# One matmul for both token parts in the last 64 key tiles, the first 64 key tiles split by GpSimd alone, and the first value parts made during the last key tile

## The chip, the cores and the metric

The kernel runs on one core of one Trainium2 chip. The metric is the device time in microseconds; lower is better. TensorE does the matmuls, VectorE (DVE) and ScalarE (ACT) the elementwise work, GpSimd (POOL) one kind of elementwise work, and SyncE (SP) issues the DMAs.

## The reference

One decoder block for 256 tokens of width 1024: a mixer (gated convolution and dilated attention), then PEER, a retrieval of single-neuron experts. The change is in PEER:

```python
def peer(xn, w_q, sub_keys, u_tab, v_tab):
    ...
        q = (xc @ w_q).reshape(TOKEN_CHUNK, PEER_HEADS, 2, half)
        s = jnp.einsum('thpd,hpnd->thpn', q, sub_keys).astype(jnp.float32)
        top_s, top_i = lax.top_k(s, PEER_TOPK)
        cand = top_s[:, :, 0, :, None] + top_s[:, :, 1, None, :]
        best_s, best_c = lax.top_k(cand.reshape(...), PEER_TOPK)
        ...
        e = i1 * PEER_N_KEYS + i2
        gate = jax.nn.softmax(best_s, axis=-1).astype(xc.dtype)
        h = jnp.einsum('thkd,td->thk', u_tab[e], xc)
        act = jax.nn.gelu(h, approximate=False) * gate
        return jnp.einsum('thk,thkd->td', act, v_tab[e])
```

There are 128 x 128 experts, each with one row of 1024 numbers in `u_tab` (its key) and one in `v_tab` (its value).

## The kernel before, in words

The kernel gathers nothing. It multiplies the tokens by all 16,384 keys, applies gelu, multiplies by a dense matrix of gates that is zero where an expert was not picked, and multiplies by all values. Keys and values come as 128 tiles each, of 128 x 1024 numbers (512 KB): 128 key tiles (the stage `U0`), then 128 value tiles (the stage `V0`). Ahead of them stand 76 tiles of the mixer and of the query projection (the front).

**Precision.** Every product of 32-bit numbers is made from parts: a weight is `hi + lo`, a token vector is `nrm_hi + nrm_lo`, and a tile's result is `hi*nrm_hi + hi*nrm_lo + lo*nrm_hi`. For each tile ACT copies `raw` to `hi` (`split_hi`, L310), and then POOL or DVE makes `lo = raw - hi` (`split_lo`, L323). `by_dve` says which: DVE takes every fourth tile up to tile 67 of the keys, and every second from there (from `G_SHARED`); POOL takes the others. `raw`, `hi` and `lo` are rings of four tiles (`RING`). A new `raw` tile is loaded when the `lo` of the tile four before is made, and `hi` of tile n+3 (`LEAD` is 3) is made after the matmuls of tile n-1, which used the same slot.

**A key tile** (`u_tile`, by `product`, L1055) is 24 matmuls of 256 columns (the 256 tokens): eight units of the 1024 dimensions, three products each. The result is 128 keys x 256 tokens in the first half of bank 4 or 5, by turns. ACT makes gelu of it into `act` (L573), and tile n+2 waits until gelu of tile n has freed the bank (`gelu_done`).

**During the first 64 key tiles** DVE picks the experts: `top_step` runs sorts (L857, L859, L862) and, per chunk of 128 tokens, one tensor of 2048 candidate sums per partition (L871) and two lookups, each of two products of 2048 elements and a sum (L881, L886, L888). The splits of `lo` that are DVE's stand between these steps in its program, at the places that `tile_of` gives.

**During the last 64 key tiles and the first 64 value tiles** the gates are made for 8 tokens at a time, 32 groups per half: DVE builds one-hot matrices (`one_hots`: `eqB` L965, `ohA` L967, `ohB` L971), TensorE multiplies them (`gates`, L1283, 16 matmuls of 64 columns ahead of every second tile), and DVE multiplies `act` by the result (`multiply`, L983). `gate_body` is DVE's loop over four tiles.

**A value tile** (`v_tile`, L1326) is 12 matmuls of 512 columns, in which the `act` tile, again in two parts, is the loaded side. ACT makes its `nrm_hi` (`a_split`, L598) and DVE its `nrm_lo` (`low_part`, L990). The two parts take the first four blocks of the arrays that held the token parts during the key tiles.

There is no scheduler: each engine runs its program in the order in which it is written, and the engines meet at semaphores. A wait holds up all that is behind it on its engine.

## Time and profile before

| | us |
|---|---|
| median of 3 runs (1066.76 to 1069.2) | 1067.68 |
| the profiled execution | 1069.04 |
| its span, first to last instruction | 1067.3 |
| TensorE busy | 1049.8 |
| DVE busy | 751.4 |
| POOL busy | 514.0 |
| ACT busy | 509.7 |

The busy time is the time in which an engine had at least one instruction under way. Matmuls overlap each other in the records, so the pace of TensorE is read from the distance between two starts and not from the duration of one. The stages lie so: front to 291, key tiles from 298 to 694 (the last 64, with gates, from 488), value tiles with gates from 694 to 888, value tiles without gates to the end. L12 is line 12 of the kernel before.

### The profile page before, as it was taken

To read this page: it belongs to the slowest core of one execution; us is meant where nothing else is said; L and a number is where in the kernel's file an instruction comes from. 1 tells how busy PE (TensorE), PEld (TensorE's weight loads), DVE (VectorE), ACT (ScalarE), POOL (GpSimd) and SP (SyncE) were. 2 spreads that over 40 slices of the span, in tenths; PEclk is the share of its full clock that TensorE was granted. 3 is DMA by queue.
4 is the path that set the end of the run, shared out by engine and by line. 5 is a ranking of instruction groups with operands and counts; after the bars stand their busy time and mean duration, and the time that the engine had idled before them with its cause. 6 is when DMAs were issued, how large, how long until landed. Compare 5 with 4: busy or idle time off the path is not lost.

```text
span 1067.3 us, 21882 instructions
## 1 busy us (share of the span) xinstructions
PE 1049.8 (98%) x7850; PEld 961.8 (90%) x7850; DVE 751.4 (70%) x1232; ACT 509.7 (48%) x798; POOL 514.0 (48%) x216
## 2 busy tenths in 40 slices
PE   8999999999999998999999999999999999999998
PEld 6999898999999998999999999978887777888886
DVE  5375868744079899918555555599999997777775
ACT  5453667545454443454444444444444444444553
POOL 3654452654646694964344333444434434444442
PEclk8999999999999998999999999999999999999999
DMA  5864342644535544465554455545554555666662
GB/s 195 267 209 139 125 149 84 216 160 141 182 133 183 191 148 166 140 214 174 167 172 158 161 173 168 166 158 177 177 172 162 177 177 178 197 196 188 190 194 97
DMA packets 52258, 181.91 MB, mean 170 GB/s; under 512 B 5851, under 2 KB 9051, under 8 KB 52092
## 3 DMA queue, kind: packets, MB, share of 16 engines
q1 hardware_dynamic: 52220, 181.41, 52.0%
q8 instruction: 24, 0.39, 0.1%
q14 instruction: 14, 0.11, 0.0%
HBM read 177.97 MB, written 3.41 MB: 170 GB/s over the span
## 4 chain that ended last, share of the span: by engine, by line
PE 91%; DVE 7%; issue 1%; ACT 1%; DMA 0%; SPq 0%; ACTq 0%; DVEq 0%
PE bank L1055 49%; PE bank L1326 33%; PE bank L1283 3%; PE bank L1136 2%; DVE lo L323 1%; PE bank L1065 1%; PE bank L1149 1%; PE bank L1263 1%; DVE gsig L829 1%; DVE prob L748 1%; DMA relx<-rel_bias 0%; DVE act L881 0%; DVE act L886 0%; DVE act L871 0%; PE bank L1243 0%
## 5 line engine op out<-in xcount | busy, mean ns | idle before, releaser
L323 POOL TENSOR_TENSOR lo<-raw,hi 128x1024 fp32r<-128x1024 f32 x202 | 511.1, 2535 | 538.5 <-ACT hi L310 538.1
L310 ACT CAST hi<-raw 128x1024 fp32r<-128x1024 f32 x332 | 347.9, 1048 | 200.9 <-PE bank L1326 189.8
L1055 PE MATMUL bank<-nrm_hi,hi 128*128 128x256 f32 x1504 | 433.4, 288 | 7.5 <-DVE lo L323 5.1
L1055 PE MATMUL bank<-nrm_lo,hi 128*128 128x256 f32 x1504 | 428.1, 285 | 0.0
L1055 PE MATMUL bank<-nrm_hi,lo 128*128 128x256 f32 x1504 | 427.9, 285 | 0.0
L1055 PEld LDWEIGHTS bank<-nrm_hi,hi 128*128 128x128 f32 x1504 | 291.1, 194 | 12.9 <-issue 7.7
L1055 PEld LDWEIGHTS bank<-nrm_lo,hi 128*128 128x128 f32 x1504 | 291.4, 194 | 0.1
L1055 PEld LDWEIGHTS bank<-nrm_hi,lo 128*128 128x128 f32 x1504 | 291.1, 194 | 0.0
L323 DVE TENSOR_TENSOR lo<-raw,hi 128x1024 fp32r<-128x1024 f32 x130 | 173.6, 1336 | 111.0 <-ACT hi L310 110.5
L990 DVE TENSOR_TENSOR nrm_lo<-act,nrm_hi 128x256 fp32r<-128x256 f32 x128 | 151.0, 1182 | 51.2 <-ACT nrm_hi L598 51.1
L1326 PE MATMUL bank<-hi,nrm_hi 128*128 128x512 f32 x512 | 160.6, 395 | 0.7 <-ACT nrm_hi L598 0.7
L1326 PE MATMUL bank<-hi,nrm_lo 128*128 128x512 f32 x512 | 158.9, 391 | 0.3 <-DVE nrm_lo L990 0.3
L1326 PE MATMUL bank<-lo,nrm_hi 128*128 128x512 f32 x512 | 158.0, 390 | 0.0
L573 ACT ACTIVATE act<-bank 128x256 f32 x128 | 49.1, 384 | 218.0 <-PE bank L1055 217.9
L1326 PEld LDWEIGHTS bank<-hi,nrm_lo 128*128 128x128 f32 x512 | 95.1, 188 | 22.9 <-DVE nrm_lo L990 3.7
L1326 PEld LDWEIGHTS bank<-lo,nrm_hi 128*128 128x128 f32 x512 | 96.1, 188 | 20.2
L1326 PEld LDWEIGHTS bank<-hi,nrm_hi 128*128 128x128 f32 x512 | 93.7, 188 | 18.7 <-issue 0.8
L983 DVE SCALAR_TENSOR_TENSOR act<-bank,act 128x512 f32 (+1 forms) x64 | 43.9, 685 | 83.6 <-PE bank L1283 83.6
L971 DVE TENSOR_TENSOR ohB<-eqB,parts 128x1024 f16<-128x1024 f16 x64 | 59.2, 925 | 0.0
L967 DVE TENSOR_TENSOR ohA<-iota_nk,keys 128x1024 f16<-128x1024 f16 x64 | 52.5, 820 | 0.0
L598 ACT CAST nrm_hi<-act 128x256 fp32r (+1 forms) x128 | 51.2, 402 | 0.1
L689 DVE SCALAR_TENSOR_TENSOR bank<-u_pad,prm,bank 128x256 f32<-128x256 f32 x116 | 46.7, 481 | 0.0
(172 smaller groups left out, 764.8 us busy)
## 6 DMA issues: line engine op xcount, KB each, us to landing
raw<-u_tiles SPq DMA_DIRECT2D x128, 512.0 KB, 3.4
raw<-v_tiles SPq DMA_DIRECT2D x128, 512.0 KB, 3.4
raw<-front SPq DMA_DIRECT2D x76, 512.0 KB, 3.4
toeplitz<-prob SPq DMA_DIRECT2D x12, 192.0 KB, 4.4
bias<-toeplitz SPq DMA_DIRECT2D x12, 128.0 KB, 4.1
resid<-x_t SPq DMA_DIRECT2D x2, 512.0 KB, 4.5
qk<-sub_keys SPq DMA_DIRECT2D x1, 1024.0 KB, 6.8
y<-act SPq DMA_DIRECT2D x2, 512.0 KB, 2.6
```

What stands on the lines that cost most here:

```text
L310: act_e.copy(hi[:, s, :], raw[:, s, :]).then_inc(hi_ready, 1)
L323: eng.tensor_tensor(lo[:, s, :], raw[:, s, :], hi[:, s, :].bitcast(F32), ALU.subtract)\
L573: a.activation(act[:, it * 4 + (base_i + j), :], bank[4 + j % 2][:, 0:T], ACT.Gelu).then_inc(gelu_done, 1)
L598: a.copy(nrm_hi[:, (base_i + j) % RING, :], act[:, it * 4 + (base_i + j), :]).then_inc(a_hi, 1)
L689: dve.scalar_tensor_tensor(out=acc[:, b, :] if w == TAPS - 1 else part_sum, in0=src, scalar=wt, in1=part_sum, op0=ALU.mult, op1=ALU.add).t ...
L967: dve.tensor_tensor(ohA[:, g % 2], every_pair(iota_nk[:, :, :], NK), at(keys[:, 0, t], NK), ALU.is_equal).then_inc(spread, 1)
L971: dve.tensor_tensor(ohB[:, g % 2].rearrange("p a i n b -> p (a i) n b"), eqB[:, g % 2].unsqueeze(2).broadcast_to([P, TOK // PAIR, 2, HALF, ...
L983: dve.scalar_tensor_tensor(out=av, in0=gv, scalar=1.0 / GATE_SCALE, in1=av, op0=ALU.mult, op1=ALU.mult)\
L990: dve.tensor_tensor(nrm_lo[:, s, :], act[:, it * 4 + (base_i + j), :], nrm_hi[:, s, :].bitcast(F32), ALU.subtract).then_inc(a_lo, 1)
L1055: ins = pe.matmul(dst, w_[:, s, u * P:(u + 1) * P], x_[:, k, :], start=first and i == 0 and p_ == 0, stop=last and i == n - 1 and p_ == 2)
L1283: ins = pe.matmul(bank[6 + g][:, q * HALF:(q + 1) * HALF], ohA[:, g, q // PAIR, :, q % PAIR], ohB[:, g, q // PAIR, i, :, q % PAIR], start= ...
L1326: ins = pe.matmul(bank[2 * c + half][:, :], a_[:, j, c * P:(c + 1) * P], v_[:, j, half * 512:(half + 1) * 512], start=False, stop=stop and ...
```

## The change

1. **Wide key tiles.** The two token parts are interleaved in one array `nrm`, so that one matmul of 512 columns makes `hi*nrm_hi` (left half of the bank) and `hi*nrm_lo` (right half). `lo*nrm_hi` is a matmul of 256 columns into the left half. This is done in the last 64 key tiles only (`wide_tile`): 8 matmuls of 512 and 8 of 256 columns instead of 24 of 256. The halves must then be added: ACT copies the right half to `half_sum` (`copy_cross`), DVE adds the left half (`add_halves`), and ACT makes gelu of the sum (`gelu_sum`). The bank of tile n is free for tile n+2 when DVE has added (`added`).
2. **Order on ACT** in these tiles: copy of tile n, gelu of tile n-1, `split_hi` of tile n+3. Before it was `split_hi` of tile n+3, then gelu of tile n.
3. **GpSimd splits** all of the first 64 key tiles of the loop (key tiles 3 to 66); DVE none of them.
4. **The turn to the values.** During the last key tile ACT makes `nrm_hi` and DVE `nrm_lo` of the first value tile (semaphore `blocks_free`), and DVE makes the first two one-hot groups of the second half in the last round of the first half instead of behind it. `eqB` has one buffer instead of two.

```diff
         raw = sb("raw", [P, RING, D])
         hi = sb("hi", [P, RING, D], F32R)
         lo = sb("lo", [P, RING, D], F32R)
-        nrm_hi = sb("nrm_hi", [P, KB, T], F32R)
-        nrm_lo = sb("nrm_lo", [P, KB, T], F32R)
+        nrm = sb("nrm", [P, KB, 2, T], F32R)
+        nrm_hi, nrm_lo = nrm[:, :, 0, :], nrm[:, :, 1, :]
...
 
         parts = sb("parts", [P, T // PAIR, 2, PAIR], F16)
         ohA = sb("ohA", [P, 2, TOK // PAIR, NK, PAIR], F16)
-        eqB = sb("eqB", [P, 2, TOK // PAIR, HALF, PAIR], F16)
+        eqB = sb("eqB", [P, TOK // PAIR, HALF, PAIR], F16)
+        half_sum = sb("half_sum", [P, 2, T])
...
         def by_dve(base, j):
 
+            if U0 + LEAD <= base + j < G_SHARED:
+                return False
             return slot_of(base, j) == 3 or (base + j >= G_SHARED and slot_of(base, j) == 1)
...
             a.wait_ge(pick_ready, 2)
-            with a.Fori(0, HALF // RING) as it:
-                for j in range(RING):
-                    split_hi(a, U0 + HALF + LEAD, it, j)
-                    gelu(HALF, it, j)
+            def copy_cross(it, j):
+
+                a.wait_ge(pe_step, it * 4 + (S_U + HALF + j + 1))
+                a.wait_ge(gelu_done, it * 4 + (HALF + j - 1))
+                a.copy(half_sum[:, j % 2, :], bank[4 + j % 2][:, T:2 * T]).then_inc(crossed, 1)
+
+            def gelu_sum(base, it, j):
+
+                a.wait_ge(added, it * 4 + (base + j + 1))
+                a.activation(act[:, it * 4 + (HALF + base + j), :], half_sum[:, (base + j) % 2, :], ACT.Gelu)\
+                 .then_inc(gelu_done, 1)
 
             def a_split(base_i, it, j):
 
                 wait(a, pe_step, it * 4 + (S_V + base_i + j - 3))
                 a.copy(nrm_hi[:, (base_i + j) % RING, :], act[:, it * 4 + (base_i + j), :]).then_inc(a_hi, 1)
 
+            def key_round(it, first=False, last=False):
+                for j in range(RING):
+                    if last and j == RING - 1:
+                        a.wait_ge(gated, GROUPS_N)
+                        a.wait_ge(blocks_free, 1)
+                        a_split(0, 0, 0)
+                    copy_cross(it, j)
+                    if not (first and j == 0):
+                        gelu_sum(-1, it, j)
+                    split_hi(a, U0 + HALF + LEAD, it, j)
+
+            key_round(0, first=True)
+            with a.Fori(1, HALF // RING - 1) as it:
+                key_round(it)
+            key_round(HALF // RING - 1, last=True)
+            gelu_sum(HALF - 1, 0, 0)
...
             for half in range(2):
-                a.wait_ge(gated, GROUPS_N * (half + 1))
-                a_split(HALF * half, 0, 0)
+                if half:
+                    a.wait_ge(gated, GROUPS_N * 2)
+                    a_split(HALF, 0, 0)
...
             for i in range(HALF):
-                if by_dve(U0 + LEAD, i):
-                    split_lo(dve, U0 + LEAD, 0, i)
                 for n, tile in enumerate(tile_of):
...
                 wait(dve, gate_mm, n - 1)
+                wait(dve, spread, n * 2)
...
-                dve.tensor_tensor(eqB[:, g % 2], every_pair(iota_nk[:, half * HALF:(half + 1) * HALF, :], HALF),
...
+
+            def add_halves(it, j):
+
+                dve.wait_ge(crossed, it * 4 + (j + 1))
+                dve.tensor_tensor(half_sum[:, j % 2, :], bank[4 + j % 2][:, 0:T], half_sum[:, j % 2, :], ALU.add)\
+                   .then_inc(added, 1)
...
 
@@ -1003,14 +1036,19 @@
                         multiply(half, it, j // 2)
                     elif not last:
                         one_hots(half, it, 2 + j // 2)
+                    elif half == 0:
+                        one_hots(1, 0, j // 2)
                     if by_dve(base + LEAD, j):
                         split_lo(dve, base + LEAD, it, j)
+                    if half == 0:
+                        if last and j == RING - 1:
+                            low_part(0, 0, 0)
+                        add_halves(it, j)
...
             for half in range(2):
-                one_hots(half, 0, 0)
-                one_hots(half, 0, 1)
-                if half == 1:
-                    low_part(0, 0, 0)
+                if half == 0:
+                    one_hots(0, 0, 0)
+                    one_hots(0, 0, 1)
                 gate_body(half, 0, first=True)
                 with dve.Fori(1, HALF // RING - 1) as it:
...
+            def wide_tile(it, j, last=False):
+
+                b = bank[4 + j % 2]
+                if isinstance(it, int) and it == 0 and j < 2:
+                    pe.wait_ge(gelu_done, HALF + j - 1)
+                else:
+                    pe.wait_ge(added, it * 4 + (j - 1))
+                wait_lo(pe, U0 + HALF, it, j)
+                for k in range(KB):
+                    unit = slice(k * P, (k + 1) * P)
+                    pe.matmul(b[:, :], hi[:, j, unit], nrm[:, k, :, :].rearrange("p a t -> p (a t)"),
+                              start=k == 0, stop=False, skip_group_check=True)
+                    ins = pe.matmul(b[:, 0:T], lo[:, j, unit], nrm_hi[:, k, :],
+                                    start=False, stop=k == KB - 1, skip_group_check=True)
+                    if last and k == RING - 1:
+                        ins.then_inc(blocks_free, 1)
+                ins.then_inc(pe_step, 1)
...
-            def u_and_gates(it):
+            def u_and_gates(it, last=False):
                 for j in range(RING):
                     if j % 2 == 0:
                         gates(0, it, j // 2)
-                    u_tile(HALF, it, j)
+                    wide_tile(it, j, last and j == RING - 1)
 
             u_and_gates(0)
-            with pe.Fori(1, HALF // RING) as it:
+            with pe.Fori(1, HALF // RING - 1) as it:
                 u_and_gates(it)
```

The order on **ACT** in the last 64 key tiles. Before, one tile and the start of the next, from the loop (`L573` is gelu, `L310` is `split_hi` of tile n+3; REGISTER_ALU and ISA rows carry waits and addresses):

```order
L310 CAST hi<-raw 128x1024 [waits pe_step,raw_in0]
L572 REGISTER_ALU
L573 ISA [waits pe_step]
L573 ACTIVATE act<-bank 128x256
L310 CAST hi<-raw 128x1024 [waits pe_step,raw_in1]
```

Of the change, the last two tiles (`L598` is the copy of tile n, `L603` gelu of the sum of tile n-1, `L312` is `split_hi` of tile n+3, `L609` is `a_split` of the first value tile):

```order
L598 COPY half_sum<-bank 128x256 [waits gelu_done,pe_step]
L603 ACTIVATE act<-half_sum 128x256 [waits added]
L312 CAST hi<-raw 128x1024 [waits pe_step,raw_in1]
L609 CAST nrm<-act 128x256 [waits pe_step,blocks_free,gated]
L598 COPY half_sum<-bank 128x256 [waits gelu_done,pe_step]
L603 ACTIVATE act<-half_sum 128x256 [waits added]
L312 CAST hi<-raw 128x1024 [waits pe_step,raw_in2]
L603 ACTIVATE act<-half_sum 128x256 [waits added]
```

`split_hi` of tile n+3 now stands behind the copy of tile n, which waits until the matmuls of tile n are done; before it waited only for those of tile n-1.

The order on **DVE** in the same tiles. Before, an even and an odd tile, the first round of `gate_body` (`L983` is `multiply`, `L323` is `split_lo` of tile n+3, then a one-hot group):

```order
L983 SCALAR_TENSOR_TENSOR act<-bank,act 128x64x8 [waits gate_mm,gelu_done]
L323 TENSOR_TENSOR lo<-raw,hi 128x1024 [waits hi_ready]
L965 TENSOR_TENSOR eqB<-iota_nk,keys 128x512 [waits gate_mm]
L967 TENSOR_TENSOR ohA<-iota_nk,keys 128x1024
L971 TENSOR_TENSOR ohB<-eqB,parts 128x1024 [waits second]
```

Of the change, an even and an odd tile (`L1010` is `multiply`, `L327` is `split_lo`, `L1023` is `add_halves`):

```order
L1010 SCALAR_TENSOR_TENSOR act<-bank,act 128x64x8 [waits gate_mm]
L327 TENSOR_TENSOR lo<-raw,hi 128x1024 [waits hi_ready]
L1023 TENSOR_TENSOR half_sum<-bank,half_sum 128x256 [waits crossed]
L992 TENSOR_TENSOR eqB<-iota_nk,keys 128x512 [waits spread,gate_mm]
L994 TENSOR_TENSOR ohA<-iota_nk,keys 128x1024
L998 TENSOR_TENSOR ohB<-eqB,parts 128x1024 [waits second]
L1023 TENSOR_TENSOR half_sum<-bank,half_sum 128x256 [waits crossed]
```

In every even tile the addition stands behind `split_lo` of tile n+3, which waits for `split_hi` of tile n+3 on ACT; in every odd tile it stands behind a one-hot group.

The order on **DVE** in the first 64 key tiles, at the two lookups of the second chunk. Before:

```order
L881 TENSOR_TENSOR act<-act,iota 128x2048 [waits chain]
L886 TENSOR_TENSOR act<-act 128x2048 [waits chain]
L888 TENSOR_REDUCE act<-act 128x128 [waits chain]
L323 TENSOR_TENSOR lo<-raw,hi 128x1024 [waits hi_ready,chain]
L881 TENSOR_TENSOR act<-act,iota 128x2048
L886 TENSOR_TENSOR act<-act 128x2048 [waits chain]
L888 TENSOR_REDUCE act<-act 128x128 [waits chain]
L916 TENSOR_TENSOR act<-act 128x128 [waits chain]
L323 TENSOR_TENSOR lo<-raw,hi 128x1024 [waits hi_ready] x2
```

Of the change, the same steps:

```order
L909 TENSOR_TENSOR act<-act,iota 128x2048 [waits chain]
L914 TENSOR_TENSOR act<-act 128x2048 [waits chain]
L916 TENSOR_REDUCE act<-act 128x128 [waits chain]
L909 TENSOR_TENSOR act<-act,iota 128x2048 [waits chain]
L914 TENSOR_TENSOR act<-act 128x2048 [waits chain]
L916 TENSOR_REDUCE act<-act 128x128 [waits chain]
L944 TENSOR_TENSOR act<-act 128x128 [waits chain]
```

The splits between the steps are gone, and with them every wait of DVE for ACT in this stage until the gates' softmax.

## Rows read from the trace of the kernel before

**Rows 1.** The page, part 4: the chain that ended last, by engine.

```profile
PE 91%; DVE 7%; issue 1%; ACT 1%; DMA 0%; SPq 0%; ACTq 0%; DVEq 0%
```

**Rows 2.** Chain in order of time, two pairs of key tiles: start, duration us.

```profile
598.87 5.83 PE bank L1055 x48
605.19 5.83 PE bank L1055 x48
```

**Rows 3.** Timeline, 404 to 424: start, duration us, engine, line [idle before <-releaser].

```profile
412.40 2.72 DVE L323 TENSOR_TENSOR lo<-raw,hi 128x1024 fp32r<-128x1024 f32 x1
...
415.26 0.55 PE L1055 MATMUL bank<-nrm_hi,hi 128*128 128x256 f32 x1 [5.10 <-DVE lo L323]
...
415.83 0.41 PE L1055 MATMUL bank<-nrm_hi,lo 128*128 128x256 f32 x1
416.04 0.41 PE L1055 MATMUL bank<-nrm_hi,hi 128*128 128x256 f32 x1
```

**Rows 4.** Windows, TensorE alone: stretch, length, busy (instructions), granted clock, DMA.

```profile
210.00:215.00 5.00, 3.70 (x31) 1.00 0.50 183
410.00:420.00 10.00, 4.90 (x24) 0.73 0.31 107
420.00:430.00 10.00, 10.00 (x80) 0.93 0.40 155
```

**Rows 5.** Timeline, POOL, DVE and ACT in the first 64 key tiles.

```profile
302.27 2.41 POOL L323 TENSOR_TENSOR lo<-raw,hi 128x1024 fp32r<-128x1024 f32 x1 [9.23 <-ACT hi L310]
...
370.85 2.29 DVE L881 TENSOR_TENSOR act<-act,iota 128x2048 f32<-128x2048 f32 x1
...
371.38 10.80 POOL L323 TENSOR_TENSOR lo<-raw,hi 128x1024 fp32r<-128x1024 f32 x3 [3.36 <-ACT hi L310]
...
373.17 4.38 DVE L886 TENSOR_TENSOR act<-act 128x2048 f32<-128x2048 f32 x1
377.59 2.29 DVE L888 TENSOR_REDUCE act<-act 128x128 f32<-128x2048 f32 x1
...
402.07 1.05 ACT L310 CAST hi<-raw 128x1024 fp32r<-128x1024 f32 x1
```

**Rows 6.** Timeline, 598 to 605.5: one pair of key tiles with gates.

```profile
598.50 0.38 ACT L573 ACTIVATE act<-bank 128x256 f32 x1 [1.56 <-PE bank L1055]
...
598.78 1.04 ACT L310 CAST hi<-raw 128x1024 fp32r<-128x1024 f32 x1
...
599.86 1.23 DVE L323 TENSOR_TENSOR lo<-raw,hi 128x1024 fp32r<-128x1024 f32 x1 [0.15 <-ACT hi L310]
...
601.00 0.42 DVE L965 TENSOR_TENSOR eqB<-iota_nk,keys 128x512 f16<-128x512 f16 x1
...
604.30 0.28 PE L1055 MATMUL bank<-nrm_lo,hi 128*128 128x256 f32 x1
...
604.42 0.28 PE L1055 MATMUL bank<-nrm_hi,lo 128*128 128x256 f32 x1
...
604.83 0.38 ACT L573 ACTIVATE act<-bank 128x256 f32 x1 [1.56 <-PE bank L1055]
...
605.03 0.36 PE L1055 MATMUL bank<-nrm_hi,hi 128*128 128x256 f32 x1
...
605.23 0.28 PE L1055 MATMUL bank<-nrm_lo,hi 128*128 128x256 f32 x1
```

**Rows 7.** Timeline, TensorE in the value tiles, merged by two.

```profile
959.93 0.62 PE L1326 MATMUL bank<-hi,nrm_hi 128*128 128x512 f32 x2
...
962.65 0.62 PE L1326 MATMUL bank<-hi,nrm_hi 128*128 128x512 f32 x2
```

**Rows 8.** Line L793, DVE adding from a bank: duration ns min/median/max.

```profile
L793 DVE TENSOR_TENSOR o_lo<-bank,o_hi x6: 415/424/425, 175.9 to 183.2; 128x256 fp32r<-128x256 f32 x6
```

**Rows 9.** Timeline, 686 to 702: the turn from keys to values.

```profile
693.11 0.66 PE L1283 MATMUL bank<-ohB,ohA 128*128 128x64 f16 x16
...
693.92 0.71 ACT L598 CAST nrm_hi<-act 128x256 fp32r<-128x256 f32 x2
...
694.47 0.70 PE L1326 MATMUL bank<-hi,nrm_hi 128*128 128x512 f32 x2 [0.71 <-ACT nrm_hi L598]
```

**Rows 10.** Waits of TensorE's loads: us in total, times, longest.

```profile
PEld bank L1326 <- DVE nrm_lo L990: 3.7, 13, 0.7
```

More of the change, by code:

```diff
@@ L268, in hybrid_block @@
         sc_ready = sem("sc_ready")
-        gelu_done = sem("gelu_done")
+        crossed, added, gelu_done = sem("crossed"), sem("added"), sem("gelu_done")
         top_done, gexp, gate_ready, pick_T, pick_ready = [sem(s) for s in (
@@ L272, in hybrid_block @@
         second, spread, gate_mm, gated = sem("second"), sem("spread"), sem("gate_mm"), sem("gated")
+        blocks_free = sem("blocks_free")
         a_hi, a_lo = sem("a_hi"), sem("a_lo")
@@ L963, in every_pair @@
                     return x.unsqueeze(1).broadcast_to([P, TOK // PAIR, m, PAIR])
-                dve.tensor_tensor(eqB[:, g % 2], every_pair(iota_nk[:, half * HALF:(half + 1) * HALF, :], HALF),
+                dve.tensor_tensor(eqB[:, :, :, :], every_pair(iota_nk[:, half * HALF:(half + 1) * HALF, :], HALF),
                                   at(keys[:, 1, t], HALF), ALU.is_equal).then_inc(second, 1)
@@ L972, in one_hots @@
                     ohB[:, g % 2].rearrange("p a i n b -> p (a i) n b"),
-                    eqB[:, g % 2].unsqueeze(2).broadcast_to([P, TOK // PAIR, 2, HALF, PAIR]),
+                    eqB[:, :, :, :].unsqueeze(2).broadcast_to([P, TOK // PAIR, 2, HALF, PAIR]),
                     parts[:, two, :, :].rearrange("p a i b -> p (a i) b").unsqueeze(2)
@@ L1310, in u_and_gates @@
                         gates(0, it, j // 2)
-                    u_tile(HALF, it, j)
+                    wide_tile(it, j, last and j == RING - 1)
             u_and_gates(0)
-            with pe.Fori(1, HALF // RING) as it:
+            with pe.Fori(1, HALF // RING - 1) as it:
                 u_and_gates(it)
+            u_and_gates(HALF // RING - 1, last=True)
             def v_tile(base_i, it, j, stop=False):
```

## The prediction

> **What bounds the kernel now.** I read the chain that ended last first: TensorE holds 91% of it and DVE 7% [rows 1]. So a change pays where it shortens TensorE's own work or takes away a wait of TensorE, and it costs where it makes one. The chain in order of time shows the stage of the change as a regular beat: two key tiles and one group of gates every 6.32 us [rows 2]. In the timeline of that stage a matmul of 256 columns starts 0.12 after the one before, so a tile is 24 x 0.12 = 2.88 us; the gates add 0.12 to 0.49 of starts and 0.08 on the second matmul behind them, 0.57 in all, and 2 x 2.88 + 0.57 is the 6.33 of the beat [rows 2, 6]. TensorE has no wait there. A matmul of 512 columns costs less for its columns: 12 of them take 2.72 us, 0.227 each [rows 7].
>
> In the first 64 key tiles the timeline shows TensorE waiting once, 5.10 us, for a split that DVE made late, behind its sorts [rows 3]. After it the matmuls start 0.21 apart instead of 0.12 [rows 3]: the granted clock is 0.73 and 0.93 of full over two stretches of 10 us, which is 6.8 us at 1.2 GHz instead of 2.4 [rows 4].
>
> **The first 64 key tiles: what goes.** The late split is no longer DVE's, so the 5.1 us wait goes. With it goes the low clock: 6.8 us at half rate do the work of 6.8 x 0.12 / 0.213 = 3.8 us, a loss of 3.0 at most; a part of it lies in the wait, and I take 2.7. Together -7.8.
>
> **The first 64 key tiles: what comes.** POOL needs 2.41 us for a split alone, inside the 2.88 of a tile [rows 5]. But it does not run alone. When DVE's product L881 started at 370.85, POOL's splits went from 371.38 to 382.18, 10.80 for three. DVE's next product L886, issued 1.79 after POOL, took 4.38, while the sum L888 took its 2.29 beside POOL [rows 5]. I read this as taking turns: a DVE product of two arrays in SBUF and a split of POOL never run together, and each product takes its 2.28 from POOL. 10.80 less what is left of L881 (1.76) and one product (2.28) leaves 6.76 for three splits, 2.25 each.
>
> The Trainium skill says the same (SBUF — State Buffer, Who interferes with whom): a DVE instruction with two SBUF inputs and a GpSimd one that reads SBUF block each other fully, and a reduction never contends. By that rule the new addition, with one input in PSUM, stays out of it; the trace agrees as far as its rows go.
>
> Until now POOL had one free slot in four tiles to catch up; it loses it. DVE's work is no longer spread out by its splits, so the products come close together. First stretch (two lookups of the first chunk, then L871): five products, 11.4 us of POOL's time, within 22.7 us (each product followed by a split, and two sums). TensorE uses 22.7 / 2.88 = 7.9 tiles in it, 7.9 x 2.40 = 19.0 of POOL. 30.4 into 22.7 leaves POOL 7.7 behind. What it may be behind: `hi` of 402.07 is ready at 403.12, a split alone would be done at 405.6, and TensorE came to that tile at 415.26 - 5.10 = 410.16: 4.5 us with the handover [rows 3, 5]. So TensorE waits 3.2. Second stretch (lookups of the second chunk): four products and small steps, 10.0, within 18; 6.25 tiles x 2.40 = 15; behind by 7.0, wait 2.5. Sum 5.7. With 2.25 for a split it is 2.0 + 1.6 = 3.6. The waits come in pieces of a split or less with matmuls between. A stretch with 1.3 of 5 us idle kept the clock at 1.00 [rows 4], so I charge no clock; if it falls in both stretches, 2 x 2.7 more. I take +5.7, bounds 3.6 and 11.
>
> **The last 64 key tiles.** TensorE's own work: a wide tile is 8 x 0.227 + 8 x 0.120 = 2.78, 0.107 less than now; the beat could be 6.11 instead of 6.32.
>
> The Trainium skill (TensorE: Matmul & The Clock Gate, Back-to-back issue gap) gives a gap of columns / 2.4 + 2.5 ns, with which eight matmuls fewer would save 20 ns a tile. The trace does not agree: 120 and 227 ns are 13 ns over the columns' time. By the page the beat could only be 6.28, and in the sum below a wide tile would be 0.09 longer, +2.7 us in all; I go by the rows.
>
> Whether TensorE keeps its pace depends on the bank. Tile n+2 waits for the addition of tile n. For an even tile the way there is, from the last matmul's start: to ACT 0.41 (604.42 to 604.83); copy of the right half, next instruction after 0.28 (598.50 to 598.78) [rows 6]; gelu of tile n-1 from SBUF, between 0.28 and half of the two casts' 0.71, I take 0.30 [rows 9]; `split_hi` 1.04; to DVE 0.04; `split_lo`, which stands ahead of the addition, 1.14 (599.86 to 601.00) [rows 6]; the addition 0.42, as L793, the same form [rows 8]; to TensorE 0.14 (415.12 to 415.26) [rows 3]. Sum 3.77. The tile itself takes 8 x 0.227 + 7 x 0.12 + 0.08 = 2.73 from its first to its last start. An even tile can follow an even tile after 6.50 us, not 6.11: TensorE would stand still for 0.39 in each pair, behind the gates. Against now that is +0.18 a pair, 31 times: +5.6. Bounds: 0.15 either way on the chain, +1 to +10.
>
> Odd tiles don't bind. DVE ends the even addition about 0.5 after the odd tile is done, the one-hots take 1.6 more, the addition 0.4, so the bank is free some 2.6 after the tile's end, and tile n+2 starts later than 3.1. Behind the waiting addition on DVE stand only the one-hots and `multiply`, which have a pair's time to spare. POOL's split of the odd tiles ends about 0.7 after the even tile's end, a microsecond before DVE's split begins, so the two don't meet. The loads from HBM (same number, same size) follow the splits, with more than 5 us in hand.
>
> **The turn and the rest.** Behind the last gates TensorE started the values after 1.36 (693.11 to 694.47), where gates alone take 0.49 [rows 6, 9]. Parts and one-hots are now ready: -0.9. The work moved into the last round (one cast, one subtraction, two one-hot groups) fills DVE where no split or one-hot of its own was due. One buffer for `eqB` costs nothing, since other work stands between two groups. In the values DVE is late now and then, 3.7 us in 13 waits of the loads [rows 10], most of it hidden; it may move by 1 either way, and I put 0.
>
> **Sum.** -7.8 + 5.7 + 5.6 - 0.9 = +2.6 on the profiled 1069.04, which lies 1.4 above the median: 1067.7 + 2.6 = 1070.2 (rounded). About 0.2%, 2.1 us, is what a measurement can tell here.
>
> **The rivals.**
> 1. The bank's chain doesn't bind. It would have to be 3.38 or less. For it: all its terms are small, and ACT and DVE are half idle; against it: each term is in a row, and the order of both programs puts two splits into it. Then -7.8 + 5.7 - 6.6 - 0.9 = -9.6: 1058. Chance 0.12.
> 2. POOL keeps up, because it gets two turns for one of DVE during the sums. For it: DVE waits for POOL too, which spreads its products. Then -5.7 on the forecast: 1064.5. Chance 0.12.
> 3. The other way: POOL's waits lower the clock in both stretches, since they lie close together: +5.4, 1075.6. It decides from a stretch in which TensorE is idle as in the 5.1 us wait. Chance 0.12.
> 4. A wide tile has the smaller saving, because a matmul of 256 columns behind one of 512 does not keep 0.12. Then +2.7, 1073. Chance 0.06.
> The forecast as worked out, 1066 to 1074, has 0.58.
>
> **How the numbers follow.** The forecast is slightly over the bound to slower; of its 0.58 I give 0.38 to slower, 0.18 to same, 0.02 to faster. Rival 1 is faster, rival 2 is faster by 0.06 and the same by 0.06, rivals 3 and 4 are slower but for 0.02. Faster 0.20, same 0.26, slower 0.54. The range 1062 to 1076 leaves out rival 1 and the far side of rival 3.
>
> **What would show it.** The beat of the key tiles with gates: 6.50 (right), 6.11 (rival 1). In each pair a wait of TensorE's wide matmul for DVE's addition, about 0.4. In the first 64 key tiles no wait of 5 us, but some four to six of 0.5 to 1.8 for POOL's `lo`, in two clusters, around 380 and 428, with the clock at 1.00. POOL busy for 90% and more of those stretches. At the turn, 0.5 from gates to values. The prediction is wrong if ACT makes `split_hi` before the copy's turn comes in practice, if additions run in less than 0.42, or if POOL's splits stay on time.

## The result, and the profile after

| | before | this kernel |
|---|---|---|
| median of 22 runs each, us | 1069.21 (1066.76 to 1074.11) | 1072.16 (1070.29 to 1076.24) |
| ratio, 95% interval | | 1.0024 [1.0013, 1.0035] |
| span of the profiled execution, us | 1067.3 | 1070.7 |

The kernel became slower by 0.24%, on the side and about by the size of the forecast (+2.6 us). Three of the terms behind the sum were off, though, and partly made up for each other. The stages, read from the first product matmul of the key tiles, from the starts of the groups of gates, and from the last instruction:

| stage, us | before | after | difference | forecast |
|---|---|---|---|---|
| first 64 key tiles (to the first gates) | 193.04 | 189.10 | -3.94 | -2.1 |
| last 64 key tiles (first gates to the 33rd) | 202.45 | 206.79 | +4.34 | +5.6 |
| turn and values with gates (33rd to 64th gates) | 189.37 | 192.32 | +2.95 | -0.9 |
| all else | 482.4 | 482.5 | +0.1 | 0 |

The page of the kernel after, parts 1 and 4, against [rows 1]:

```profile
PE 1051.4 (98%) x7338; PEld 930.2 (87%) x7338; DVE 757.8 (71%) x1280; ACT 530.5 (50%) x862; POOL 551.2 (51%) x232
PE 79%; issue 8%; DVE 5%; ACT 4%; POOL 3%; DVEq 1%; DMA 0%; ACTq 0%; SPq 0%; POOLq 0%
```

TensorE's share of the chain fell from 91% to 79%: other engines now stand in it, POOL between 364 and 426 in the first 64 key tiles, ACT and DVE all through the last 64. The waits of TensorE, its matmuls first, then its loads (us in total, times, longest):

```profile
PE bank L1093 <- POOL lo L327: 3.1, 4, 1.3
...
PE bank L1383 <- DVE nrm L1017: 1.6, 3, 0.8
...
PE bank L1325 <- DVE half_sum L1023: 0.4, 2, 0.2
```

```profile
PEld bank L1383 <- DVE nrm L1017: 10.4, 33, 1.3
```

The second row looks small, and so does the third; the beats tell more. Gates are shown busy for 0.66 us, though the next matmul can start 0.50 after their start (693.56 and 694.06 below), so most of a wait behind gates does not appear as idle time.

**First 64 key tiles.** Timeline, TensorE's four waits for POOL (idle time in brackets):

```profile
376.96 0.48 PE L1093 MATMUL bank<-nrm,hi 128*128 128x256 f32 x2 [1.28 <-POOL lo L327]
...
386.15 0.47 PE L1093 MATMUL bank<-nrm,hi 128*128 128x256 f32 x2 [0.32 <-POOL lo L327]
...
421.19 0.47 PE L1093 MATMUL bank<-nrm,hi 128*128 128x256 f32 x2 [0.25 <-POOL lo L327]
...
425.58 0.48 PE L1093 MATMUL bank<-nrm,hi 128*128 128x256 f32 x2 [1.28 <-POOL lo L327]
```

and POOL, then DVE's products of a lookup, in the first of the two stretches:

```profile
357.17 47.75 POOL L327 TENSOR_TENSOR lo<-raw,hi 128x1024 fp32r<-128x1024 f32 x16 [0.61 <-ACT hi L312]
```

```profile
363.42 2.29 DVE L916 TENSOR_REDUCE act<-act 128x128 f32<-128x2048 f32 x1
365.74 4.43 DVE L909 TENSOR_TENSOR act<-act,iota 128x2048 f32<-128x2048 f32 x1
370.20 4.38 DVE L914 TENSOR_TENSOR act<-act 128x2048 f32<-128x2048 f32 x1
374.62 2.29 DVE L916 TENSOR_REDUCE act<-act 128x128 f32<-128x2048 f32 x1
```

POOL works 47.75 us without a gap, 2.98 a split, where it needs 2.41 alone [rows 5] and TensorE uses a tile in 2.88. The products take 4.4 and the sums 2.29, as in [rows 5]. The waits come in two clusters, around 380 and 423, four in all.

**Last 64 key tiles.** Timeline of one pair, ACT and then DVE, against [rows 6]:

```profile
600.32 0.37 ACT L598 COPY half_sum<-bank 128x256 f32<-128x256 f32 x1 [1.76 <-PE bank L1327]
600.59 0.42 ACT L603 ACTIVATE act<-half_sum 128x256 f32 x1
600.90 1.04 ACT L312 CAST hi<-raw 128x1024 fp32r<-128x1024 f32 x1
...
606.82 0.37 ACT L598 COPY half_sum<-bank 128x256 f32<-128x256 f32 x1 [1.80 <-PE bank L1327]
```

```profile
601.98 1.23 DVE L327 TENSOR_TENSOR lo<-raw,hi 128x1024 fp32r<-128x1024 f32 x1 [2.44 <-ACT hi L312]
603.12 0.42 DVE L1023 TENSOR_TENSOR half_sum<-bank,half_sum 128x256 f32<-128x256 f32 x1
```

TensorE's wide matmul starts behind it at 603.67. From the copy: 0.27 to gelu, 0.31 to `split_hi`, 1.08 to `split_lo`, 1.14 to the addition, 0.55 to TensorE, then 3.15 for the tile and the handover to the next copy: 6.50. DVE was idle for 2.44 before its split, so it was not overloaded; it stood at the wrong wait.

**The turn and the values.** Timeline at the turn, TensorE, then DVE, against [rows 9]:

```profile
693.56 0.66 PE L1339 MATMUL bank<-ohB,ohA 128*128 128x64 f16 x16
694.06 0.70 PE L1383 MATMUL bank<-hi,nrm 128*128 128x512 f32 x2
...
696.07 1.21 PE L1383 MATMUL bank<-hi,nrm 128*128 128x512 f32 x4 [0.85 <-DVE nrm L1017]
```

```profile
695.60 0.42 DVE L1017 TENSOR_TENSOR nrm<-act,nrm 128x256 fp32r<-128x256 f32 x1
695.94 0.42 DVE L1023 TENSOR_TENSOR half_sum<-bank,half_sum 128x256 f32<-128x256 f32 x1
697.20 1.37 DVE L1017 TENSOR_TENSOR nrm<-act,nrm 128x256 fp32r<-128x256 f32 x1 [0.85 <-ACT nrm L609]
```

The values do start 0.50 after the gates, not 1.36. But TensorE stops again four matmuls later: `nrm_lo` of the first value tile stands behind the second one-hot group on DVE and comes at 696. Then the loop, POOL and DVE:

```profile
743.08 2.53 POOL L327 TENSOR_TENSOR lo<-raw,hi 128x1024 fp32r<-128x1024 f32 x1 [3.62 <-ACT hi L312]
749.21 2.54 POOL L327 TENSOR_TENSOR lo<-raw,hi 128x1024 fp32r<-128x1024 f32 x1 [3.60 <-ACT hi L312]
```

```profile
742.14 1.21 DVE L327 TENSOR_TENSOR lo<-raw,hi 128x1024 fp32r<-128x1024 f32 x1
743.27 2.62 DVE L1017 TENSOR_TENSOR nrm<-act,nrm 128x256 fp32r<-128x256 f32 x1
...
749.42 2.62 DVE L1017 TENSOR_TENSOR nrm<-act,nrm 128x256 fp32r<-128x256 f32 x1
```

DVE has no idle time here and needs 6.15 a pair. In it, `low_part` takes 2.62 where it takes 0.42 alone [its row at 695.60]: it starts 0.19 behind a split of POOL and ends 0.28 behind it. TensorE could do a pair in 6.05.

### The profile page after: what moved, and what is told of

Read it like the earlier page. It is cut to its first block, busy times and chain, and to the rows that moved or that the text cites. A ratio compares the mean times of both kernels' runs of the same rounds, so it can differ in the third digit from the quotient of the medians.

```text
span 1070.7 us, 21144 instructions
## 1 busy us (share of the span) xinstructions
PE 1051.4 (98%) x7338; PEld 930.2 (87%) x7338; DVE 757.8 (71%) x1280; ACT 530.5 (50%) x862; POOL 551.2 (51%) x232
## 4 chain that ended last, share of the span: by engine, by line
PE 79%; issue 8%; DVE 5%; ACT 4%; POOL 3%; DVEq 1%; DMA 0%; ACTq 0%; SPq 0%; POOLq 0%
PE bank L1383 32%; PE bank L1093 28%; PE bank L1325 7%; PE bank L1327 3%; ACT hi L312 3%; POOL lo L327 3%; PE bank L1174 2%; PE bank L1339 2%; DVE half_sum L1023 1%; PE bank L1103 1%; PE bank L1187 1%; PE bank L1301 1%; DVE nrm L1017 1%; DVE gsig L857 1%; DVE prob L776 1%
## 5 line engine op out<-in xcount | busy, mean ns | idle before, releaser
L327 POOL TENSOR_TENSOR lo<-raw,hi 128x1024 fp32r<-128x1024 f32 x218 | 548.3, 2525 | 504.7 <-ACT hi L312 504.4
L312 ACT CAST hi<-raw 128x1024 fp32r<-128x1024 f32 x332 | 347.5, 1047 | 202.1 <-PE bank L1383 191.0
L1093 PE MATMUL bank<-nrm,hi 128*128 128x256 f32 x1984 | 363.5, 286 | 5.4 <-POOL lo L327 3.1
L1093 PEld LDWEIGHTS bank<-nrm,hi 128*128 128x128 f32 x1984 | 312.0, 194 | 11.3 <-issue 3.4
L1383 PE MATMUL bank<-hi,nrm 128*128 128x512 f32 x1024 | 285.3, 395 | 1.6 <-DVE nrm L1017 1.6
L1093 PE MATMUL bank<-nrm,lo 128*128 128x256 f32 x992 | 282.2, 284 | 0.0
L327 DVE TENSOR_TENSOR lo<-raw,hi 128x1024 fp32r<-128x1024 f32 x114 | 144.1, 1264 | 135.8 <-ACT hi L312 135.7
L1383 PEld LDWEIGHTS bank<-hi,nrm 128*128 128x128 f32 x1024 | 187.4, 188 | 45.8 <-DVE nrm L1017 10.4
L1017 DVE TENSOR_TENSOR nrm<-act,nrm 128x256 fp32r<-128x256 f32 x128 | 180.8, 1414 | 50.0 <-ACT nrm L609 50.0
L1093 PEld LDWEIGHTS bank<-nrm,lo 128*128 128x128 f32 x992 | 192.1, 194 | 0.0
L1325 PE MATMUL bank<-nrm,hi 128*128 128x512 f32 x512 | 184.1, 403 | 3.4 <-DVE half_sum L1023 0.4
L1383 PE MATMUL bank<-lo,nrm 128*128 128x512 f32 x512 | 158.4, 390 | 0.0
L1327 PE MATMUL bank<-nrm,lo 128*128 128x256 f32 x512 | 143.1, 279 | 0.0
L1325 PEld LDWEIGHTS bank<-nrm,hi 128*128 128x128 f32 x512 | 96.1, 188 | 28.6 <-issue 3.6
L1383 PEld LDWEIGHTS bank<-lo,nrm 128*128 128x128 f32 x512 | 96.1, 188 | 20.3
L1327 PEld LDWEIGHTS bank<-nrm,lo 128*128 128x128 f32 x512 | 96.7, 189 | 0.0
L598 ACT COPY half_sum<-bank 128x256 f32<-128x256 f32 x64 | 23.8, 372 | 95.9 <-PE bank L1327 95.9
L609 ACT CAST nrm<-act 128x256 fp32r (+1 forms) x128 | 51.2, 402 | 0.0
```

The costliest lines, as they stand in the source:

```text
L312: act_e.copy(hi[:, s, :], raw[:, s, :]).then_inc(hi_ready, 1)
L327: eng.tensor_tensor(lo[:, s, :], raw[:, s, :], hi[:, s, :].bitcast(F32), ALU.subtract)\
L609: a.copy(nrm_hi[:, (base_i + j) % RING, :], act[:, it * 4 + (base_i + j), :]).then_inc(a_hi, 1)
L1017: dve.tensor_tensor(nrm_lo[:, s, :], act[:, it * 4 + (base_i + j), :], nrm_hi[:, s, :].bitcast(F32), ALU.subtract).then_inc(a_lo, 1)
L1093: ins = pe.matmul(dst, w_[:, s, u * P:(u + 1) * P], x_[:, k, :], start=first and i == 0 and p_ == 0, stop=last and i == n - 1 and p_ == 2)
L1325: pe.matmul(b[:, :], hi[:, j, unit], nrm[:, k, :, :].rearrange("p a t -> p (a t)"), start=k == 0, stop=False, skip_group_check=True)
```

## The experiments

All are compared with runs of the kernel before on the same chip. Stages are read as in the table above. The start of the first key tile moves by up to 3 us from one profile to another, so spans are not compared, stages are.

### The addition ahead of the split, and POOL alone with the splits

**e1.** In every even tile DVE adds before it splits:

```diff
-                    if by_dve(base + LEAD, j):
-                        split_lo(dve, base + LEAD, it, j)
                     if half == 0:
                         if last and j == RING - 1:
                             low_part(0, 0, 0)
                         add_halves(it, j)
+                    if by_dve(base + LEAD, j):
+                        split_lo(dve, base + LEAD, it, j)
```

> The changed kernel with one line moved: in every even key tile DVE adds the halves before it makes the lo of tile n+3, not behind it. My theory: the bank of an even tile comes free through copy, gelu, split of hi, split of lo and addition, 3.77 us, and that chain sets the beat of 6.50 us a pair. With the addition first the chain is copy and addition alone, about 1.4 us, TensorE sets the beat at 6.11, and the stage is 12 us shorter: ratio to before about 0.991, 1060 us. Rival: the beat is set by something else that comes to 6.50 as well (the copies on ACT, or DVE's whole work in a pair): then the beat stays at 6.4 or more and the time moves by under 2 us.

Measured: 1063.41 us, ratio 0.9931 [0.9905, 0.9957]; last 64 key tiles 196.27, every beat 6.13 or 6.14, the other stages as in the changed kernel within 0.3. Timeline, DVE:

```profile
603.06 0.42 DVE L1023 TENSOR_TENSOR half_sum<-bank,half_sum 128x256 f32<-128x256 f32 x1 [1.18 <-ACT half_sum L598]
604.32 1.23 DVE L327 TENSOR_TENSOR lo<-raw,hi 128x1024 fp32r<-128x1024 f32 x1 [0.83 <-ACT hi L312]
```

The addition now follows the copy of 602.66 by 0.40 instead of 2.80. The chain of the even tiles was the cost, and nothing else in that stage was: 10.5 us lie in the order of two instructions, where 12 were expected.

**e2.** The kernel before, with the third part of the change alone:

```diff
         def by_dve(base, j):
 
+            if U0 + LEAD <= base + j < G_SHARED:
+                return False
...
             for i in range(HALF):
-                if by_dve(U0 + LEAD, i):
-                    split_lo(dve, U0 + LEAD, 0, i)
```

> The kernel before with one part of the change alone: POOL makes every lo of key tiles 3 to 66, DVE none. The two profiles put the first gates 3.9 us earlier in the changed kernel (486.8 against 490.7). My theory: this part gives that alone, 3.9 us less in all, ratio 0.996, with about four waits of TensorE for POOL's lo, 3 us in sum, clock at 1.00. Rival: what is won is given back in the value tiles, since DVE comes to them in another state: ratio 1.000 within 0.001.

Measured: 1064.82 us, ratio 0.9956 [0.9939, 0.9974]; first 64 key tiles 189.10, four waits for POOL's `lo`, 3.2 us together, clock 1.00 throughout the stretch. The gain of this part stands alone, and the rest of its kernel is as before (202.45 and 189.34), the beats of the value tiles too. So what the changed kernel loses in the values comes from the other parts of the change.

### How much the lock costs in the first half

The lock is what the prediction calls taking turns: a product of DVE with two inputs in SBUF and a split of POOL don't run together.

**e7.** In six of the eight products of the lookups DVE works on an eighth of the elements (the first chunk's first lookup keeps its size), so the picked experts are not the reference's:

```diff
+                    n = PH * TOPK if (c, w) == (0, 0) else TOPK
...
+                    h = PH if (c, w) == (0, 0) else 1
+                    link(dve.tensor_tensor(e4[:, 0:h], e4[:, 0:h], tf[:, 0:h], ALU.mult))
```

> The changed kernel with six of the eight large products of DVE's lookups cut to an eighth of their size (the first lookup keeps its size; the picked experts are then not those of the reference). It shows what POOL's waits for these products cost in the first 64 key tiles. My theory: the products hold POOL up for 2.28 us each, so with them gone TensorE's waits for POOL's lo, 3.1 us in four pieces in the changed kernel, fall to 0.5 or less, and the stage from the first key tile to the first gates takes 186.0 to 186.5 instead of 189.1. Rival: POOL is late because of all its splits together or because of the loads behind them: then 188.5 or more.

Measured, one run: 1068.37; first 64 key tiles 185.03 instead of 189.10, and no wait for POOL's `lo`. The cost of POOL as the only splitter is DVE's products in its way: 4.07 us.

### The turn

**e3.** `nrm_lo` of the first value tile and the last addition ahead of the second one-hot group:

```diff
                     elif half == 0:
+                        if j == RING - 1:
+                            low_part(0, 0, 0)
+                            add_halves(it, j)
                         one_hots(1, 0, j // 2)
...
```

> The changed kernel with the last key tile's work on DVE in another order: the nrm_lo of the first value tile and the addition of the last key tile stand before the second one-hot group, not behind it. After the change the value tiles with gates took 199.4 us against 195.5, at a beat of 6.15 instead of 6.05. Theory A: DVE is the bound of that stage at 6.15 a pair; before, it came into the stage with a lead of about 2 us that lasted for 21 pairs; the change spends the lead at the turn, where DVE stands idle for 1.7 us and TensorE waits 0.85. With the new order TensorE does not wait at the turn and DVE has 1.7 us of lead more: the value stage takes 197 us or less, time 2 to 3 us less, ratio to before about 1.000. Rival B: the beat of 6.15 comes from the position of POOL's splits against DVE's, not from a lead: only the 0.85 at the turn goes, ratio 1.0016.

**e4.** e1 and e3 together.

> The addition first in every key tile and the new order at the turn, both. If the two effects are apart they add: 12 and 2 to 3 us less than the changed kernel, about 1057 us, ratio to before 0.989. If the faster key tiles bring DVE later into the value stage (it has less idle time at a beat of 6.11), a part of it is given back there: 1059 to 1060.

Measured: e3 1072.34, ratio 1.0028 [1.0010, 1.0045], values with gates 193.49; e4 1060.62, ratio 0.9908 [0.9883, 0.9934], 196.26 for the last 64 key tiles and 191.82 for the values. As a cure e3 failed. Timeline of e3, POOL, DVE and TensorE:

```profile
693.31 2.41 POOL L327 TENSOR_TENSOR lo<-raw,hi 128x1024 fp32r<-128x1024 f32 x1 [4.00 <-ACT hi L312]
693.35 2.91 DVE L998 TENSOR_TENSOR ohB<-eqB,parts 128x1024 f16<-128x1024 f16 x1
...
696.19 2.56 DVE L1017 TENSOR_TENSOR nrm<-act,nrm 128x256 fp32r<-128x256 f32 x1
698.80 1.65 PE L1385 MATMUL bank<-hi,nrm 128*128 128x512 f32 x3 [3.16 <-DVE nrm L1017]
```

The one-hot product and then `nrm_lo` of the second value tile each landed behind a split of POOL, and TensorE waited 3.16 us; 3.4 us of low clock followed at 698.8. But what came then told more than the cure would have: 20 beats of 6.05 to 6.08, and 6.15 only after them. The kernel before has the same (behind a first beat of 6.90, 20 beats of 6.05 or 6.06, then 6.09 to 6.19), while the changed kernel has 6.15 from the third beat on. A lead of DVE would hide its pace in this way, at 0.10 a pair. That DVE's pace was 6.15 in the fast beats too can be read in the kernel before, in whose timeline two runs of `multiply` lie 6.15 apart while TensorE's beat is 6.05:

```profile
744.20 0.68 DVE L983 SCALAR_TENSOR_TENSOR act<-bank,act 128x512 f32 x1
...
750.35 0.68 DVE L983 SCALAR_TENSOR_TENSOR act<-bank,act 128x512 f32 x1
```

e4 has the same order at the turn as e3, but its wait there is 0.74 us and not 3.16, and it has no fast beats: 6.11 to 6.20 from the third on. The order of e3 alone builds no lead.

### The values: which work stands behind POOL

**e5.** In the second half DVE multiplies in the odd tiles, ahead of `low_part`, so that POOL's split meets `multiply` first, which has one input in PSUM, and `low_part` later:

```diff
+                    if half == 1 and j % 2:
+                        multiply(half, it, j // 2)
                     if half == 1 and not (last and j == RING - 1):
                         low_part(1, it, j)
                     if j % 2 == 0:
-                        multiply(half, it, j // 2)
+                        if half == 0:
+                            multiply(half, it, j // 2)
```

> The changed kernel with DVE's multiply of the value tiles moved from ahead of the even tile's split of lo to behind it, just ahead of the odd tile's nrm_lo. In the trace of the changed kernel that nrm_lo takes 2.6 us instead of 0.4, since POOL's split is under way; multiply reads a bank and runs beside POOL (0.61). Theory A (DVE is the bound of the value tiles with gates at 6.15 a pair, 2.2 of it behind POOL): the wait swallows multiply, DVE's round is 5.54, TensorE sets the beat at 6.05 in all pairs but the first two, the 32 groups take 189.5 instead of 192.3, time 2.8 less: ratio to before 1.000. Rival C: POOL's split starts when TensorE and ACT let it, so DVE waits for its end wherever multiply stands, or another DVE step is caught instead: beat 6.15 stays, ratio 1.0025.

**e6.** e1 and e5 together. **e8.** e6, with `low_part(0, 0, 0)` ahead of the second one-hot group.

> The addition first in the key tiles and multiply under POOL's lock in the value tiles, both. By theory A the gains add: 10.5 in the key tiles and 2.8 in the value tiles less than the changed kernel, about 1059 to 1060.6 us, ratio to before 0.991. By rival C only the first: 0.993.

> As the kernel with addition first and multiply under the lock, and at the turn DVE makes the nrm_lo of the first value tile before the second one-hot group, the addition of the last key tile staying behind it. TensorE's wait of 0.57 for that nrm_lo goes. By theory A it is 0.6 less than the kernel without, or nothing if the chain from the last addition to the second value tile holds TensorE up by as much. Ratio to before 0.990.

Measured: e5 1068.13, ratio 0.9984 [0.9969, 1.0000], values with gates 189.13 instead of 192.32; e6 1057.53, 0.9890 [0.9869, 0.9911], 188.68; e8 1057.26, 0.9880 [0.9861, 0.9898], 188.61. Timeline of e5, POOL and DVE:

```profile
747.33 2.39 POOL L327 TENSOR_TENSOR lo<-raw,hi 128x1024 fp32r<-128x1024 f32 x1 [3.66 <-ACT hi L312]
```

```profile
746.89 0.68 DVE L1010 SCALAR_TENSOR_TENSOR act<-bank,act 128x512 f32 x1
747.49 2.52 DVE L1017 TENSOR_TENSOR nrm<-act,nrm 128x256 fp32r<-128x256 f32 x1
```

The beats are 6.03 to 6.07 from the third on, to the end. `low_part` is still behind POOL, for 2.52, but POOL's split starts at 747.33, 0.24 before `multiply` is done, and runs beside it that long. In the changed kernel the whole 2.4 us of the split and all else of DVE's round came one after the other, 6.15; 0.1 less was enough to fit into TensorE's 6.05. A round of 5.54, as expected, is not seen: DVE has no idle time in e5 either, since `low_part` still lasts until the split is done, and the split comes by TensorE's pace (POOL waits for `hi`, and ACT for TensorE). That DVE's pace is what TensorE kept in the changed kernel is shown by the beats. Doing `nrm_lo` earlier on top of that (e8) brings nothing that can be measured.

### Splits for DVE at chosen places

Three kernels give DVE a few splits of the first half back, each behind the sum of a lookup, on top of e8. They differ in the tiles only:

```diff
+        DVE_TAKES = {(0, 2): 23, (0, 5): 27, (1, 2): 39, (1, 5): 43}
...
                         lookup(c, *divmod(r - PH // 2 - 2, 3))
+                        if (c, r - PH // 2 - 2) in DVE_TAKES:
+                            split_lo(dve, U0 + LEAD, 0, DVE_TAKES[c, r - PH // 2 - 2])
```

(23 is key tile 26, since the numbers begin at tile 3.) **e9** is as shown; **e10** leaves out the last; **e11** has 42 (key tile 45) in the third place instead of 39 (key tile 42), and no fourth.

> This is the kernel with additions first, the multiply moved and the low part early, and in it DVE makes four of the first 64 splits again: key tiles 26, 30, 42 and 46, each behind the sum of a lookup (L916), that is where POOL has just lost its turns to DVE's products. Theory (POOL falls behind through the lock, by what the products take from it): POOL has 2.4 us less to do in each place, 4.8 in each of the two stretches in which it fell behind by some 4 to 5, so TensorE's waits for POOL's lo (3.1 us in four) go but for at most 0.5, and the first 64 key tiles take 185.0 to 186.0 instead of 189.1, as with the small products; time 1057.3 - 3.5 = 1053.8, ratio 0.985. Rival (POOL is behind for another reason, such as ACT's order or the loads, or DVE's split itself waits for ACT's hi and then comes late for TensorE, as in the kernel before): the stretch stays within 188 to 191, with waits of TensorE for DVE's lo in place of POOL's; time 1057 to 1059.

> As the kernel with four splits given to DVE, but key tile 46 stays with POOL, so DVE makes tiles 26, 30 and 42. In the run with four, TensorE had no wait for POOL left and one of 2.7 us for DVE's split of tile 46, which DVE could only start at 432.15, behind two lookups, while POOL stood idle for 7.04 us; the granted clock fell to 0.91 over the stretch 420 to 440. Theory (POOL's waits are the lock's, and the last split only came too late): POOL makes tile 46 by 428, the wait and the low clock go, the first 64 key tiles take 185.0 to 186.0 instead of 189.45, time 1058.4 - 3.9 = 1054.5, ratio 0.985. Rival (each place given to DVE or POOL brings one such wait): a wait of 1.3 us or more for POOL's lo comes back near 430, and the stretch stays at 187.5 or more, time 1056.5 or more.

> As the kernel with three splits given to DVE, but in the third place DVE makes key tile 45 instead of 42. In the run with 42, TensorE waited 2.72 us at 421.56 for that split: DVE comes to this place at about 419.8, when TensorE is already at tile 42, and its split takes 3.3 there. TensorE comes to tile 45 only at about 427.3. Theory (waits of POOL's lo are the lock's; the two misses were DVE's splits set too late for their tile): no wait for lo of 0.5 us or more, clock 1.00, first 64 key tiles 185.0 to 186.0 instead of 189.3, time 1058.4 - 3.5 = 1054.9 or a little less, ratio 0.985. Rival (DVE behind POOL's lock is always late for somebody in the second stretch): a wait of 1 us or more stays between 415 and 435, and the stretch takes 187 or more, time 1056.5 or more.

| | first 64 key tiles, us | time | ratio |
|---|---|---|---|
| e9 | 189.45 | 1058.37 | 0.9887 [0.9866, 0.9909] |
| e10 | 189.32 | 1059.68 | 0.9899 [0.9879, 0.9920] |
| e11 | 185.03 | 1053.46 | 0.9845 [0.9822, 0.9868] |

e9 and e10 missed. All waits for POOL went, but one for DVE came. Waits of TensorE in e9, and in e10 the wait in the timeline and the window 420 to 430 (length, busy time of TensorE, its loads, DVE, ACT and POOL, granted clock, DMA share, GB/s):

```profile
PE bank L1103 <- DVE lo L329: 2.7, 1, 2.7
```

```profile
421.56 0.77 PE L1103 MATMUL bank<-nrm,hi 128*128 128x256 f32 x2 [2.72 <-DVE lo L329]
```

```profile
420.00:430.00 10.00, 8.44 (x59) 8.47 (x60) 9.93 (x4) 2.57 (x5) 6.05 (x3) 0.83 0.59 210
```

The wait of e9 at 423.24 is the same one, 123.9 us behind the first key tile in both: it is for key tile 42, the third split, and not for tile 46, as the expectation of e10 has it. So e10 took away a split that did no harm. Each lost the 2.7 us and, with the clock down, another 1.5 or so, as much as the four waits had cost. In e11 the third split is due late enough:

```profile
421.98 3.12 DVE L329 TENSOR_TENSOR lo<-raw,hi 128x1024 fp32r<-128x1024 f32 x1 [0.27 <-ACT hi L312]
```

It ends at 425.1, TensorE has no wait for a `lo` left, and the stage takes 185.03, the same as with the small products. e11 is the fastest kernel of all, 1.5% below the kernel before.

## Why the prediction was right, and where it was not

**The bank's chain: right.** "An even tile can follow an even tile after 6.50 us" was worked out from rows of before; the pair shown above has 6.50, term by term within 0.05. Rival 1 (the chain doesn't bind) fell, and e1 shows that the chain is the cause and its price. The total was +4.34 instead of +5.6, because the first two beats were free (6.13) and the other 30 were 6.48 on average. The free beat was put at 6.11 and is 6.13: by its own terms (24 x 0.120 against 8 x 0.227 + 8 x 0.120) a wide tile saves 0.104 and not 0.107, and e1's beats show 0.097.

**Rival 4: fell.** A pair of a 512-column and a 256-column matmul starts 0.35 after the pair before it, as the rows said (0.347). The gap that the Trainium skill gives for a single matmul (TensorE: Matmul & The Clock Gate, Back-to-back issue gap) would by the prediction's estimate have left a beat of 6.28; e1's is 6.13.

**The first 64 key tiles: both terms had the right sign, the second was too large.** What goes was put at -7.8 and is -8.0 (193.04 to the 185.03 of e11 and e7, both without any wait). What comes was put at +5.7 and is +4.07 (e7); 3.1 of that are the four waits, and about 0.23 more goes with each: across the wait of 1.28 at 376.96 two matmuls start 1.56 apart where 0.12 is due, and the next one comes 0.07 late. The lower bound of 3.6, with 2.25 for a split, was nearer than the 2.40 that I took; which part of the backlog's sum was too large was not tried apart. The lock itself was right: with small products it costs nothing, and the sums (L916) ran in their 2.29. That a reduction stays out of it is also what the Trainium skill states (SBUF — State Buffer, Who interferes with whom). Rival 2 (POOL keeps up) and rival 3 (its waits lower the clock) fell: the clock was 1.00.

**The turn: right and spent at once.** The forecast -0.9 is there (0.50 instead of 1.36 from gates to values). TensorE then waits 0.85 and 0.46 for `nrm_lo`.

**The values: the step that failed.** "It may move by 1 either way, and I put 0", from the 3.7 us of waits in [rows 10]. It moved by 3.8: the stage was put at -0.9, for the turn, and is +2.95. Those waits were not spread over the stage: in the timeline of the kernel before, the first and the last of the 13 are these, one a pair, and the first comes after 20 pairs:

```profile
816.30 0.30 PEld L1326 LDWEIGHTS bank<-hi,nrm_lo 128*128 128x128 f32 x2 [0.17 <-DVE nrm_lo L990]
...
889.98 0.30 PEld L1326 LDWEIGHTS bank<-hi,nrm_lo 128*128 128x128 f32 x2 [0.74 <-DVE nrm_lo L990]
```

DVE's round was 6.15 in the kernel before too. There DVE stands idle for the last time three pairs behind the turn; from then on its one-hots come 0.10 closer to their gates with each pair, for 18 pairs (apart from one step of 2.3, where POOL's split moves ahead of them), and when these 1.8 us are used up TensorE's waits begin. In the changed kernel DVE has no idle time from the second pair on, and TensorE meets DVE's pace from the third beat on, which costs 1.8 us, behind two longer beats at the turn (7.22 and 6.84 instead of 6.90 and 6.06), 1.1 us, in which the 0.86 won from gates to values are already counted.

That a lead is what differed rests on these distances and on e3, where 20 fast beats came back behind a stop of 3.16 us and the low clock after it; that DVE's round is the limit rests on e5, where a shorter round made them all fast. What built the lead in the kernel before was not tried apart. TensorE's stop at the turn does not explain it alone: it was 0.71 us there with 20 fast beats, and 0.74 in e4 with none. The timelines show one difference behind the turn. In the kernel before, neither `nrm_lo` of the first pair stood behind a split of POOL, and DVE was idle for 1.17 us after them; in the changed kernel one did:

```profile
697.25 0.41 DVE L990 TENSOR_TENSOR nrm_lo<-act,nrm_hi 128x256 fp32r<-128x256 f32 x1
...
699.12 0.42 DVE L990 TENSOR_TENSOR nrm_lo<-act,nrm_hi 128x256 fp32r<-128x256 f32 x1
```

```profile
700.23 2.62 DVE L1017 TENSOR_TENSOR nrm<-act,nrm 128x256 fp32r<-128x256 f32 x1
```

Such a meeting takes 2.2 us, a little more than the lead. In e3 the first pair behind the stop has none either, in e4 it has one. That this is the cause is argued from the timelines and not shown.

**The total: in part luck.** The first 64 key tiles came out 1.8 below their forecast and the last 64 1.3 below, the values 3.8 above. A forecast of +2.6 against a measured +2.95 is closer than its terms were.

## What to carry to other kernels

When an engine runs nearly as long a round as the one that it feeds, look at the beats over the whole stage and not at the sum of waits: waits that begin late in a stage say that a lead is running out, and a change ahead of the stage can take that lead away. When a result is needed by the bound engine, put the instruction that frees it ahead of every instruction that waits for something else; here the order of two instructions was worth 10.5 us, where the whole change moved the time by 3. Work given to an engine behind others must be due later than the engine can come to it, not only be short.

## What the runs showed of the hardware

- Around a wait of TensorE of 2.7 us (e9, e10) or 3.16 us (e3) the granted clock shows 3.4 us at the lower of its two levels, around the 5.10 us wait of before 6.8 us, part of them within the wait; the four waits of 0.25 to 1.28 us left the granted clock at 1.00. Where the clock fell, a wait cost about half as much again (4.3 us in all for the 2.7 of e10, 8.0 for the 5.10).
- POOL and DVE take turns also where the DVE instruction is small: `low_part` (0.42 alone) takes 2.5 to 2.6 us if it starts just behind a split of POOL, and a one-hot product in f16 2.9 instead of 0.69 (e3 at 693.35, the kernel before at 741.04). The sums, with one input, and `multiply`, with one in PSUM, kept their 2.29 and 0.68 beside POOL.
